# Root of the norm applied to the results in six norms, spread modulation units, loads reordered at the start, mix heads with scaling ahead and one recurrence chunk per head

## The chip, the core and the metric

One core of one Trainium2 chip runs the whole program in one launch. The metric is the time of an execution in device microseconds (us). Five engines work from instruction streams of their own and wait for one another through semaphores: TensorE (PE; its weight loads are PEld), VectorE (DVE), ScalarE (ACT), GpSimd (POOL) and SyncE (SP), which here issues every DMA.

## The reference

256 tokens of width 1024 in float32 pass two networks one after the other. The first has two layers of: a SwiGLU feed-forward block; a mixing block (a gated linear recurrence of 1024 channels beside forgetting attention with 8 heads of 128, merged by sigmoid gates); a second SwiGLU block; and a gated projection of a side input ("PLE"). Each of the four starts with an RMS norm:

```python
def rms_norm(x, g):
    xf = x.astype(jnp.float32)
    y = xf * lax.rsqrt(jnp.mean(xf * xf, axis=-1, keepdims=True) + EPS)
    return (y * g.astype(jnp.float32)).astype(x.dtype)

for i in range(DEPTH):                       # DEPTH = 2
    x = x + 0.5 * swiglu_ffn(rms_norm(x, ffn1_norm[i]), ffn1_w_in[i], ffn1_w_out[i])
    h = rms_norm(x, mix_norm[i])
    ...
    merged = jax.nn.sigmoid(ga + mb_a) * ya + jax.nn.sigmoid(gb + mb_b) * yb
    x = x + merged @ w_o[i]
    x = x + 0.5 * swiglu_ffn(rms_norm(x, ffn2_norm[i]), ffn2_w_in[i], ffn2_w_out[i])
    gate = jax.nn.sigmoid(rms_norm(x, ple_norm[i]) @ ple_w_gate[i] + ple_b_gate[i])
    x = x + gate * (p[i] @ ple_w_proj[i])
```

The second network (two layers on 256 tokens and, at first, 256 context tokens) has feed-forward blocks, a convolution block and windowed attention. Its norms are scaled, shifted and gated by modulation vectors: silu(c) times the matrices ada_w, of 1024 x 9216 for each layer. These products depend on no token, so the kernel does them along the way.

## The kernel before, in words

Activations lie transposed, channels on partitions and tokens along the free axis: Xx is x as 8 chunks (kc) of 128 channels x 256 tokens. The weights are cut into **units** of 256 output columns, 1 MB each (the loop variable u, with u.k its number). A float32 product is made of three: a weight w is split into wh (ACT copies raw to the reduced format, L1048, helper hi) and wl = raw - wh (DVE, L1443, helper lo), an activation likewise into Hh and Hl (or Fh and Fl), and PE adds wh*Hh, wh*Hl and wl*Hh (L560 to L562, helper linear). A unit has two tiles t of 128 columns, and for 256 tokens takes 48 matmuls of 256 columns.

raw has four slots, filled by SP in the order of units; wh and wl have two buffers, by the unit's parity, so hi(u+2, t) waits until PE has done tile t of unit u. The results of a unit are in two banks of PSUM, again by parity.

The order on each engine is written out by hand: every engine has one straight program, and in it each unit is a turn, with hi(u+2), lo(u+2) placed around what the engine does with the results of u.

- A **feed-forward** block is 34 units in three groups: 8, 8 and 6 units G (gate and up columns side by side) each followed by 4 units O (down projection). For a unit G, ACT takes the tanh of the gate tile (L1118), DVE multiplies (L1436, L1520) into Pp, ACT and DVE split that into Fh and Fl (L1129, L1536).
- A **norm** comes between blocks. ACT squares x by pairs of chunks, DVE adds them, PE sums over channels with a matrix of ones (L596), ACT takes the square root (L1091), DVE the reciprocal (L1453), PE spreads it over partitions (L617) into PSUM bank 4. Then, chunk by chunk, DVE writes x * gain * root (L1436), ACT copies it to Hh (L1103), DVE makes Hl (L1481), and PE's first unit of the next block starts with the first chunk.
- Modulation is done in 18 **batches** of 4 units of ada_w. Each takes 16 matmuls (L634) straight from raw. In the kernel before, a batch sits at one place: eight of the first nine in a norm (norm_sums), around the sums and the root, or at the first head; their 4 MB take all four slots of raw, and the next block's second unit (Unit(after + 1), "held") is loaded and split only after them. Before the first one, c has to be turned and passed through silu.
- The **mix heads**: 8 steps st. In each, PE does tile 0 of a unit of the merge gates, head_values(st - 2) (L803), spread(st) (L783: the inverse norms of q and k of head st, spread over partitions into bank 4), tile 1, turn_probs(st - 1) (L769) and head_scores(st) (L793 to L795). DVE scales Q and K of head st by bank 4 (L1733, L1734; semaphore qkn_done), masks and takes maxima of the scores (L1737 to L1744), normalises after ACT's exp (L1216), and in steps 0 to 3 runs the recurrence of two chunks: multiply (L1436), scan (L1759), times the gelu gate (L1762; y_done), ACT copies to Fh (L1236), DVE makes Fl (L1766). ACT ends the step with the tanh of the merge gates (L1240) and begins the next with hi.

```python
for st in range(HEADS):                                   # PE, L800 on
    u = Unit(k + 20 + st)
    linear(u, part(Hh, T), part(Hl, T), T, tiles=(0,))
    ...
    spread(st)
    linear(u, part(Hh, T), part(Hl, T), T, tiles=(1,))
    if st >= 1:
        turn_probs(st - 1)
    head_scores(st)
```

- **PLE** is four pairs of units: a gate unit and a projection unit (2 chunks deep, 12 matmuls). ACT takes the gate's tanh from PSUM (L1275), DVE combines gate and projection and adds to x (L1436 twice), ACT squares x for the next norm (L1081).
- At the **start** SP issues the tokens, then 28 loads of parameters, then the weights.

Of the kernel before, what the change touches and what calls it, by code (L numbers as in the profile page):

```python
# [33 lines left out]
P = 128  # L34
T = 256
# [35 lines left out]
BATCH_AFTER = tuple(k for l in range(DEPTH) for k in ((K_LAYER,) if l else ()) + (  # L71
    l * K_LAYER + K_MIX, l * K_LAYER + K_GATES, l * K_LAYER + K_FFN2, l * K_LAYER + K_PLE)) + (
    K_SECOND, K2_CONV, K2_CONV + 4, K2_PW2, K2_FFN2, K2_L1, K2_KV, K2_KV + 5, K2_FFN4)
assert BATCH * len(BATCH_AFTER) == 2 * MOD_UNITS


def batches_before(k):
    return sum(after < k for after in BATCH_AFTER)


class Unit:
# [3 lines left out]
    def __init__(self, k):  # L85
        self.k = k
        self.slot = k % 4
        self.par = k % 2
        self.raw = k + BATCH * batches_before(k)
# [7 lines left out]
    def held(self):  # L97

        return self.k - 1 in BATCH_AFTER or self.k == K2_WO + 1
# [4 lines left out]


    def batch_member(self):

        b = batches_before(self.k) - 1
        return (b, self.k - BATCH_AFTER[b] - 1) if b >= 0 and self.k - BATCH_AFTER[b] <= BATCH else None

    def raw_free(self):
        return 2 * self.k + 2
# [22 lines left out]
class ModUnit:  # L135
# [3 lines left out]
    def __init__(self, b, m):  # L139
        self.b, self.m = b, m  # L140
        self.place = BATCH_AFTER[b] + 1 + m
        self.raw = self.place + BATCH * b
        self.slot = self.raw % 4
        self.l, self.index = divmod(BATCH * b + m, MOD_UNITS)
# [4 lines left out]
    def raw_free(self):  # L149
        return Unit(self.place).raw_free()  # L150

    def done(self):
        return BATCH * self.b + self.m + 1

# [51 lines left out]
def build(nc, A, out):  # L206
# [12 lines left out]
    with ctx:  # L219
# [43 lines left out]
        tiny = sb("tiny", [P, 64])  # L263
        S1 = sb("S1", [P, 3, C, 2])
# [42 lines left out]
        sqa_done = sem("sqa_done")  # L307
        rs_done, rb_done = sem("rs_done"), sem("rb_done")
# [70 lines left out]

        def head_row(what, h):  # L380
# [3 lines left out]
        def mod_bank(b):  # L384

            return 7 if BATCH_AFTER[b] in (K_GATES, K_LAYER + K_GATES, K2_CONV + 4, K2_KV + 5) else 5

        def mod_rows(b):

            if BATCH_AFTER[b] == K2_KV + 5:  # L390
                return Vb[:, 1, 0:T]
            return Ss[:, T:2 * T] if BATCH_AFTER[b] in (K_GATES, K_LAYER + K_GATES) else Rr[:, T:2 * T]
# [5 lines left out]
        def _(sp):  # L398
# [11 lines left out]
            for r, name in ((R_FFN1, "ffn1_norm"), (R_MIX, "mix_norm"), (R_MERGE, "merge_b"), (R_CONVB, "conv_b"),  # L410
# [1665 lines left out]
```

## Time and profile before

| | us |
|---|---|
| median of 3 runs | 3329.41 (3328.5 to 3331.13) |
| the profiled execution's own time | 3330.55 |
| its span | 3328.8 |
| PE busy in the span | 3181.1 (96%) |
| PE weight loads busy | 2799.8 (84%) |
| DVE busy | 1913.6 (57%) |
| ACT busy | 1346.4 (40%) |
| mean granted clock of TensorE | 0.975 |

The span is what the profiler recorded from first to last instruction; the execution's own time is 1.75 us more. Busy time is the sum over an engine's instructions, overlaps counted once. A matmul counts as busy at whichever of the two clocks it runs, so a share of 96% does not say that 4% is all there is to gain.

### The profile page before, as it was taken

To read this page: it belongs to the slowest core of one execution; us is meant where nothing else is said; L and a number is where in the kernel's file an instruction comes from. 1 tells how busy PE (TensorE), PEld (TensorE's weight loads), DVE (VectorE), ACT (ScalarE), POOL (GpSimd) and SP (SyncE) were. 2 spreads that over 40 slices of the span, in tenths; PEclk is the share of its full clock that TensorE was granted. 3 is DMA by queue.
4 is the path that set the end of the run, shared out by engine and by line. 5 is a ranking of instruction groups with operands and counts; after the bars stand their busy time and mean duration, and the time that the engine had idled before them with its cause. 6 is when DMAs were issued, how large, how long until landed. Compare 5 with 4: busy or idle time off the path is not lost.

```text
span 3328.8 us, 49855 instructions
## 1 busy us (share of the span) xinstructions
PE 3181.1 (96%) x21085; PEld 2799.8 (84%) x21085; DVE 1913.6 (57%) x2983; ACT 1346.4 (40%) x2046; POOL 2.3 (0%) x6
## 2 busy tenths in 40 slices
PE   7999899998999899998999999899999999999999
PEld 7999799998998889997888866578887888874898
DVE  5567656556557666556434379853335433455555
ACT  4445344445444444445322242432223222337544
POOL 0000000000000000000000000000000000000000
PEclk8999899999999999998999999999999999999999
DMA  6675437666665537657333343253334333242563
GB/s 194 181 209 159 159 126 213 185 195 199 188 201 173 180 102 208 187 166 220 102 102 89 89 127 101 88 140 89 102 92 124 114 89 101 89 140 76 165 184 108
DMA packets 671175, 478.86 MB, mean 144 GB/s; under 512 B 21487, under 2 KB 670057, under 8 KB 670953
## 3 DMA queue, kind: packets, MB, share of 16 engines
q1 hardware_dynamic: 670953, 475.68, 47.8%
q8 instruction: 166, 2.72, 0.3%
q14 instruction: 56, 0.46, 0.0%
HBM read 474.57 MB, written 1.05 MB: 143 GB/s over the span
## 4 chain that ended last, share of the span: by engine, by line
PE 80%; DVE 10%; ACT 4%; DVEq 3%; DMA 1%; issue 1%; SPq 0%; ACTq 0%
PE ps L560 24%; PE ps L562 24%; PE ps L561 24%; DVE Pp L1436 3%; DVE wl L1443 3%; DVEq L1895 2%; ACT wh L1048 2%; PE ps L634 1%; PE ps L999 1%; DMA raw<-in_ada_w 1%; DVEq L1486 1%; PE ps L976 1%; DVE Hl L1436 1%; PE ps L617 1%; ACT L1060 1%
## 5 line engine op out<-in xcount | busy, mean ns | idle before, releaser
L1443 DVE TENSOR_TENSOR wl<-raw,wh 128x1024 fp32r<-128x1024 f32 x780 | 951.2, 1224 | 920.2 <-ACT wh L1048 919.5
L1048 ACT ACTIVATE wh<-raw 128x1024 fp32r<-128x1024 f32 x780 | 816.5, 1057 | 1477.6 <-PE ps L562 1410.6
L560 PE MATMUL ps<-Hh,wh 128*128 128x256 f32 (+1 forms) x4048 | 1305.1, 322 | 44.4 <-DVE Hl L1436 13.8
L562 PE MATMUL ps<-Hh,wl 128*128 128x256 f32 (+1 forms) x4048 | 1287.3, 318 | 0.0
L561 PE MATMUL ps<-Hl,wh 128*128 128x256 f32 (+1 forms) x4048 | 1287.1, 318 | 0.0
L560 PEld LDWEIGHTS ps<-Hh,wh 128*128 128x128 f32 x4048 | 785.7, 194 | 111.0 <-issue 37.8
L561 PEld LDWEIGHTS ps<-Hl,wh 128*128 128x128 f32 x4048 | 786.1, 194 | 49.6 <-issue 2.4
L562 PEld LDWEIGHTS ps<-Hh,wl 128*128 128x128 f32 x4048 | 784.8, 194 | 48.2
L560 PE MATMUL ps<-Fh,wh 128*128 128x256 f32 (+1 forms) x1824 | 582.0, 319 | 13.2 <-DVE Fl L1805 7.7
L561 PE MATMUL ps<-Fl,wh 128*128 128x256 f32 (+1 forms) x1824 | 580.7, 318 | 0.0
L562 PE MATMUL ps<-Fh,wl 128*128 128x256 f32 (+1 forms) x1824 | 580.6, 318 | 0.0
L560 PEld LDWEIGHTS ps<-Fh,wh 128*128 128x128 f32 x1824 | 348.9, 191 | 37.6 <-DVE Fl L1805 8.2
L562 PEld LDWEIGHTS ps<-Fh,wl 128*128 128x128 f32 x1824 | 349.0, 191 | 23.4
L561 PEld LDWEIGHTS ps<-Fl,wh 128*128 128x128 f32 x1824 | 349.0, 191 | 23.2
L1520 DVE TENSOR_TENSOR Pp<-Ss,ps 128x256 f32<-128x256 f32 (+1 forms) x176 | 91.8, 521 | 157.1 <-PE ps L562 154.3
L1436 DVE SCALAR_TENSOR_TENSOR Pp<-Vb,par,Pp 128x512 f32<-128x512 f32 x155 | 109.8, 748 | 6.7 <-issue 0.9
L1436 DVE SCALAR_TENSOR_TENSOR Xx<-ps,G,Xx 128x256 f32<-128x256 f32 x112 | 52.3, 479 | 90.1 <-PE ps L562 90.0
L1129 ACT ACTIVATE Fh<-Pp 128x256 fp32r<-128x256 f32 (+1 forms) x176 | 85.0, 483 | 30.3 <-DVE Pp L1520 30.3
L1536 DVE TENSOR_TENSOR Fl<-Pp,Fh 128x256 fp32r<-128x256 f32 (+1 forms) x176 | 91.2, 518 | 0.0
L1436 DVE SCALAR_TENSOR_TENSOR Ss<-Tt,ps 128x256 f32<-128x256 f32 (+1 forms) x176 | 90.6, 515 | 0.0
L634 PE MATMUL ps<-raw,cs 128*32 128x256 f32 x1152 | 72.8, 393 | 10.8 <-DMA raw<-in_ada_w 10.8
L1118 ACT ACTIVATE Tt<-ps 128x256 f32<-128x256 f32 (+1 forms) x176 | 78.5, 446 | 0.0
(273 smaller groups left out, 1895.4 us busy)
## 6 DMA issues: line engine op xcount, KB each, us to landing
raw<-in_ffn_w_in SPq DMA_DIRECT2D x176, 512.0 KB, 5.2
raw<-in_ffn_wi SPq DMA_DIRECT2D x176, 512.0 KB, 5.2
raw<-in_ada_w SPq DMA_DIRECT2D x144, 512.0 KB, 4.5
raw<-in_w_in SPq DMA_DIRECT2D x112, 512.0 KB, 4.8
raw<-in_ffn_w_out SPq DMA_DIRECT2D x64, 512.0 KB, 4.3
raw<-in_ffn_wo SPq DMA_DIRECT2D x64, 512.0 KB, 4.3
raw<-in_ffn_w_out SPq DMA_DIRECT2D x32, 384.0 KB, 3.5
raw<-in_ffn_wo SPq DMA_DIRECT2D x32, 384.0 KB, 3.6
```

The costliest lines, as they stand in the source:

```text
L560: nc.tensor.matmul(o, wh[:, u.par, kc, w], xh(kc), start=(kc == 0), stop=False)
L561: nc.tensor.matmul(o, wh[:, u.par, kc, w], xl(kc), start=False, stop=False)
L562: return nc.tensor.matmul(o, wl[:, u.par, kc, w], xh(kc), start=False, stop=(kc == kc_n - 1))
L634: mm = nc.tensor.matmul(ps[32 * j:32 * j + 32, mod_bank(b), 0:256], cs[:, kc, 2 * (BATCH - 1 - m):2 * (BATCH - 1 - m) + 32], raw[:, u.slot ...
L1048: nc.scalar.activation(tile_of(wh[:, u.par], t), tile_of(raw[:, u.slot], t), ACT.Copy) \
L1118: nc.scalar.activation(Tt[:, u.par, 0:n], bank(u, 0, n), ACT.Tanh, scale=0.5) \
L1129: nc.scalar.activation(dst, src, ACT.Copy).then_inc(fh_done, 1)
L1436: return V.scalar_tensor_tensor(out=o, in0=in0, scalar=scalar, in1=in1, op0=op0, op1=op1)
L1443: V.tensor_tensor(tile_of(wl[:, u.par], t), tile_of(raw[:, u.slot], t), tile_of(wh[:, u.par], t).bitcast(F32), ALU.subtract).then_inc(lo_d ...
L1520: V.tensor_tensor(Pp[:, u.par, 0:n], Ss[:, 0:n], bank(u, 1, n), ALU.mult) \
L1536: V.tensor_tensor(o, p, h.bitcast(F32), ALU.subtract).then_inc(f_done, 1)
L1895: dve.drain()
```

## The change

Six things are changed; nothing in the second network's blocks is, but for names.

1. **Six norms deferred** (0, 2, 3 of each layer's 0 to 3, that is the norms ahead of both feed-forward blocks and of PLE; the norm ahead of mix stays). The split is made of x * gain without the root: ACT unscaled_high (two copies with a scale, after each pair's squares), DVE unscaled_low (two instructions, a turn later). PE begins the next block on these; the sums go ahead of chunk 4 of its first unit and the spreading of the root ahead of chunk 7 (norm_between). ACT copies the root to SBUF, and DVE multiplies results by it: in each unit G two more multiplications (before the tanh, and before the product), in PLE one per gate unit. PLE's tanh now reads what DVE wrote (L2015).
2. **Modulation units spread**: five of the first nine batches go as single units between units of the feed-forward blocks (MEMBER_AT), their copy, turn and keep one, two and three units after the last.
3. **Start**: one load of ffn1's gains as a column (gain0, 4-byte elements), then the weights of units 0 to 3, then the parameters; PE turns the parameters after unit 1, DVE copies them before unit 2, and c is prepared before unit 4.
4. **PLE's side input** is turned and split during the last group of the feed-forward block before it.
5. **Mix heads, scaling ahead**: spread(st + 1) stands after tile 1 of step st, ahead of turn_probs and head_scores(st).
6. **Recurrence**: one chunk in each of the eight steps in place of two in each of the first four; its Fl a step later (scanned_low), the last one after the steps.

```diff
+def batch_places():
+    out = []
+    for l in range(DEPTH):
+        k = l * K_LAYER
+        out.append(tuple(k + j for j in ((3, 5, 7, 9) if l else (8, 10, 13, 15))))
+        if l:
+            out.append(tuple(k + j for j in (15, 17, 19, 21)))
+        out += [(k + K_MIX,) * BATCH, (k + K_GATES,) * BATCH, tuple(k + K_FFN2 + j for j in (3, 5, 7, 9))]
...
+            with nc.allow_non_contiguous_dma(reason="a column of gains"):
+                sp.dma_start(gain0[:], A["ffn1_norm"][0].rearrange("(c p) -> p c", p=P)).then_inc(gain_in, 16)
...
+                        if u.k == 4:
+                            load_params()
...
                     linear(u, part(Hh, T), part(Hl, T), T, tiles=(0,))
...
-                    spread(st)
+                    if st == 0:
+                        spread(0)
                     linear(u, part(Hh, T), part(Hl, T), T, tiles=(1,))
+                    if st + 1 < HEADS:
+                        spread(st + 1)
                     if st >= 1:
                         turn_probs(st - 1)
                     head_scores(st)
...
+            def last_add(norm_i, i, u):
+
+                hi(u.later(2), 0)
+                if i == 3:
+                    squares(norm_i, i, T, u)
+                    unscaled_high(norm_i, i)
+                    hi(u.later(2), 1)
+                else:
+                    hi(u.later(2), 1)
+                    squares(norm_i, i, T, u)
+                    unscaled_high(norm_i, i)
...
-                    if st < 4:
-                        for j in (2 * st, 2 * st + 1):
-                            act.wait_ge(y_done, l * C + (j + 1))
-                            nc.scalar.activation(Fh[:, 0, j, :], Pp[:, j % 2, T:2 * T], ACT.Copy).then_inc(yh_done, 1)
+                    act.wait_ge(y_done, l * C + (st + 1))
+                    nc.scalar.activation(Fh[:, 0, st, :], Pp[:, st % 2, T:2 * T], ACT.Copy).then_inc(yh_done, 1)
...
                     hi(u.later(2), 0)
-                    hi(u.later(2), 1)
-                    act.wait_ge(mm_done, u.mm_done(1))
+                    act.wait_ge(banks_free[u.par], u.read_out())
                     for t in range(2):
                         r = R_PLEB + 2 * j + t
-                        ins = nc.scalar.activation(Pp[:, j % 2, t * T:(t + 1) * T], bank(u, t, T), ACT.Tanh, scale=0.5,
-                                                   bias=half[:, r:r + 1])
-                    ins.then_inc(banks_free[u.par], 1)
+                        a = Pp[:, j % 2, t * T:(t + 1) * T]
+                        ins = nc.scalar.activation(a, a, ACT.Tanh, scale=0.5, bias=half[:, r:r + 1])
+                    ins.then_inc(ple_tanh, 1)
+                    hi(u.later(2), 1)
...
+                            r = inverse_root(norm)
+                            dve.wait_ge(mm_done, u.mm_done(0))
+                            V.tensor_tensor(Ss[:, 0:n], bank(u, 0, n), r, ALU.mult).then_inc(a_done, 1)
+                            lo(u.later(2), 0)
+                            done = fi * FC + g * 8
+                            dve.wait_ge(tanh_done, done + (i + 1))
+                            stt(Ss[:, 0:n], Tt[:, u.par, 0:n], 1.0, Ss[:, 0:n], ALU.add, ALU.mult)
+                            dve.drain()
+                            V.tensor_tensor(Ss[:, 0:n], Ss[:, 0:n], r, ALU.mult)
+                            dve.drain()
+                            dve.wait_ge(mm_done, u.mm_done(1))
+                            V.tensor_tensor(Pp[:, u.par, 0:n], Ss[:, 0:n], bank(u, 1, n), ALU.mult) \
+                                .then_inc(banks_free[u.par], 1)
...
-                        for j in two_chunks:
-                            V.tensor_tensor_scan(Pp[:, j % 2, 0:T], decay[:, j, :], Xc[:, j, :], 0.0, ALU.mult, ALU.add)
...
+                    V.tensor_tensor_scan(Pp[:, st % 2, 0:T], decay[:, st, :], Xc[:, st, :], 0.0, ALU.mult, ALU.add)
+                    dve.drain()
+                    V.tensor_tensor(Pp[:, st % 2, T:2 * T], Pp[:, st % 2, 0:T], Gb[:, st, :], ALU.mult) \
+                        .then_inc(y_done, 1)
+                    if st >= 1:
+                        scanned_low(st - 1)
+                scanned_low(HEADS - 1)
```

What moves on the engines, at the two places that matter most. Each row is one instruction: line, operation, written and read tiles, shape of the output, and what it waits for.

PE in a head step, from the end of tile 1 of the merge-gate unit to tile 0 of the next. Before (L769 turns the probabilities, L793 to L795 are the scores):

```order
L562 MATMUL ps<-Hh,wl 128x256
L769 MATMUL ps<-co,Tt 128x128 [waits pn_done]
L769 MATMUL ps<-co,Tt 128x128 x2
L793 MATMUL ps<-QK 128x128 [waits qkn_done]
L794 MATMUL ps<-tt_r,picks 128x128
```

and with the change (L881 is spread, L867 turn_probs, L891 the scores):

```order
L615 MATMUL ps<-Hh,wl 128x256
L881 MATMUL ps<-rqs,picks 128x256 [waits qkn_done]
L881 MATMUL ps<-rqs,picks 128x256 x3
L867 MATMUL ps<-co,Tt 128x128 [waits pn_done]
L867 MATMUL ps<-co,Tt 128x128 x2
L891 MATMUL ps<-QK 128x128 [waits qkn_done]
```

The wait for qkn_done now stands ahead of the four spreading matmuls and of the turning, where it stood behind the turning.

ACT in head step 5, between the tanh of two merge gates. Before (L1048 is hi, L1211 head_out, L1207 the turned probabilities, L1216 exp):

```order
L1240 ACTIVATE Gb<-ps,half 128x256
L1048 ACTIVATE wh<-raw 128x8x128 [waits mm_done,raw_full1]
L1211 ACTIVATE Fh<-ps 128x256 [waits pv_done]
L1048 ACTIVATE wh<-raw 128x8x128 [waits mm_done]
L1207 ACTIVATE Tt<-ps 128x384 [waits tr_done]
L1216 ACTIVATE Tt,tiny<-Tt,tiny 128x128 [waits nmax_done]
L1216 ACTIVATE Tt,tiny<-Tt,tiny 128x256
L1240 ACTIVATE Gb<-ps,half 128x256 [waits mm_done]
```

and with the change:

```order
L1380 ACTIVATE Gb<-ps,half 128x256
L1142 ACTIVATE wh<-raw 128x8x128 [waits mm_done,raw_full1]
L1353 ACTIVATE Fh<-ps 128x256 [waits pv_done]
L1142 ACTIVATE wh<-raw 128x8x128 [waits mm_done]
L1349 ACTIVATE Tt<-ps 128x384 [waits tr_done]
L1358 ACTIVATE Tt,tiny<-Tt,tiny 128x128 [waits nmax_done]
L1358 ACTIVATE Tt,tiny<-Tt,tiny 128x256
L1376 ACTIVATE Fh<-Pp 128x256 [waits y_done]
```

The copy of the recurrence's result (L1376), with its wait for y_done, now stands ahead of the merge gates' tanh in steps 4 to 7 too, where nothing stood; in steps 0 to 3 it is one copy in place of two.

## Rows read from the trace of the kernel before

**Rows 1.** The page: busy engines; waits of PE: total, times, longest

```profile
PE 3181.1 (96%) x21085; PEld 2799.8 (84%) x21085; DVE 1913.6 (57%) x2983; ACT 1346.4 (40%) x2046; POOL 2.3 (0%) x6
...
PE ps L634 <- DMA raw<-in_ada_w: 10.8, 8, 4.8
```

**Rows 2.** Stretches: length, busy PE, PEld, DVE, ACT, POOL (instructions), clock, DMA share, GB/s

```profile
0.00:28.55 28.55, 8.73 (x65) 7.70 (x66) 11.73 (x28) 9.25 (x13) 2.30 (x6) 0.73 0.82 217
28.55:33.30 4.75, 4.75 (x22) 4.75 (x23) 4.29 (x11) 2.08 (x5) 0.00 (x0) 0.50 0.63 151
36.40:210.00 173.60, 173.60 (x1449) 173.60 (x1448) 104.89 (x139) 77.86 (x108) 0.00 (x0) 1.00 0.64 185
389.10:467.40 78.30, 70.96 (x470) 64.88 (x469) 51.79 (x131) 33.29 (x77) 0.00 (x0) 0.90 0.30 97
440.40:467.40 27.00, 27.00 (x201) 24.85 (x201) 16.25 (x42) 13.09 (x30) 0.00 (x0) 1.00 0.35 118
1156.20:1232.60 76.40, 68.60 (x471) 62.29 (x470) 51.87 (x132) 33.19 (x77) 0.00 (x0) 0.93 0.33 107
538.40:554.30 15.90, 13.01 (x157) 11.12 (x157) 9.37 (x22) 8.45 (x16) 0.00 (x0) 0.89 1.05 271
738.80:783.40 44.60, 38.44 (x357) 34.86 (x360) 31.24 (x44) 26.86 (x41) 0.00 (x0) 0.96 0.61 193
783.40:804.90 21.50, 16.27 (x157) 13.33 (x156) 11.81 (x28) 10.25 (x20) 0.00 (x0) 0.76 1.05 283
```

**Rows 3.** Timeline of PE at the start (start, us, engine, line, tiles); DMA issues

```profile
6.40 3.46 PE L686 MATMUL ps<-co,QK 128*128 128x128 f32 x16 [6.40 <-DMA QK<-in_x]
...
wf<-in_w_in SPq DMA_DIRECT2D x2, 32.0 KB, 5.2
```

**Rows 4.** The chain that ended last: start, us, engine, line; two modulation units

```profile
538.40 1.86 PE ps L634 x32
```

**Rows 5.** Timeline of ACT and DVE in PLE of layer 0, pairs 2 and 3

```profile
775.01 0.82 ACT L1275 ACTIVATE Pp<-ps,half 128x256 f32<-128x256 f32 x2
775.72 2.00 ACT L1048 ACTIVATE wh<-raw 128x1024 fp32r<-128x1024 f32 x2
780.04 0.63 ACT L1081 ACTIVATE Tt<-Xx 128x512 f32<-128x512 f32 x1 [2.31 <-DVE Xx L1436]
...
778.55 0.68 DVE L1436 SCALAR_TENSOR_TENSOR Ss<-Pp,ps 128x512 f32<-128x512 f32 x1
```

**Rows 6.** Timeline of DVE in a unit G: first instruction of its turn

```profile
58.01 1.23 DVE L1443 TENSOR_TENSOR wl<-raw,wh 128x1024 fp32r<-128x1024 f32 x1 [1.38 <-ACT wh L1048]
```

**Rows 7.** Timeline of DVE and ACT, head step 3 and the start of step 4

```profile
428.56 0.29 DVE L1737 TENSOR_TENSOR Tt<-ps,co 128x128 f32<-128x128 f32 x1 [1.93 <-PE ps L795]
...
431.23 0.17 DVE L1752 RECIPROCAL tiny<-tiny 128x2 f32<-128x2 f32 x1 [0.39 <-ACT Tt L1216]
...
431.94 1.26 DVE L1759 TENSOR_TENSOR_SCAN Pp<-decay,Xc 128x256 f32<-128x256 f32 x2
433.28 0.76 DVE L1762 TENSOR_TENSOR Pp<-Pp,Gb 128x256 f32<-128x256 f32 x2
...
436.20 1.23 DVE L1443 TENSOR_TENSOR wl<-raw,wh 128x1024 fp32r<-128x1024 f32 x1 [1.25 <-ACT wh L1048]
...
440.42 0.29 DVE L1737 TENSOR_TENSOR Tt<-ps,co 128x128 f32<-128x128 f32 x1 [0.59 <-PE ps L795]
...
433.74 0.75 ACT L1236 ACTIVATE Fh<-Pp 128x256 fp32r<-128x256 f32 x2 [2.54 <-DVE Pp L1762]
434.40 0.82 ACT L1240 ACTIVATE gateA<-ps,half 128x256 f32<-128x256 f32 x2
```

**Rows 8.** Timeline of PE in a head step: the spreading

```profile
443.84 0.71 PE L783 MATMUL ps<-rqs,picks 128*128 128x256 f32 x4
```

**Rows 9.** Busy time by stretch: a wait of PE among the heads, and what follows

```profile
422.70:425.50 2.80, 0.03 (x1) 0.00 (x0) 2.22 (x5) 2.14 (x4) 0.00 (x0) 1.00 0.00 0
425.50:428.50 3.00, 2.95 (x9) 1.84 (x9) 1.13 (x1) 0.00 (x0) 0.00 (x0) 0.57 0.24 55
438.50:440.30 1.80, 1.80 (x8) 1.15 (x8) 1.23 (x1) 0.45 (x2) 0.00 (x0) 1.00 0.00 0
```

More of the change, by code:

```diff
@@ L70, with ring_order @@
 BATCH = 4
[L71 to L78, printed above, removed]
+def batch_places():
[6 more added lines that the diff above has]
+        out += [(k + K_MIX,) * BATCH, (k + K_GATES,) * BATCH, tuple(k + K_FFN2 + j for j in (3, 5, 7, 9))]
+    return out + [(k,) * BATCH for k in (
+        K_SECOND, K2_CONV, K2_CONV + 4, K2_PW2, K2_FFN2, K2_L1, K2_KV, K2_KV + 5, K2_FFN4)]
+BATCHES = batch_places()
+PLACES = [k for places in BATCHES for k in places]
+assert len(PLACES) == 2 * MOD_UNITS and PLACES == sorted(PLACES)
+BATCH_AT = {places[0]: b for b, places in enumerate(BATCHES) if places[0] == places[-1]}
+SPREAD = {b: places for b, places in enumerate(BATCHES) if places[0] != places[-1]}
+MEMBER_AT = {k: (b, m) for b, places in SPREAD.items() for m, k in enumerate(places)}
+P_TURN_AT, P_HIGH_AT, P_LOW_AT = ({l * K_LAYER + K_FFN2 + j: l for l in range(DEPTH)} for j in (26, 28, 29))
+COPY_AT = {places[-1] + 1: b for b, places in SPREAD.items()}
+TURN_AT = {places[-1] + 2: b for b, places in SPREAD.items()}
+KEEP_AT = {places[-1] + 3: b for b, places in SPREAD.items()}
+def ring_order():
+    out = []
+    for k in range(K2_END):
+        out.append((k, None))
+        out += [(None, i) for i, place in enumerate(PLACES) if place == k]
+    return out
+RING = ring_order()
+RAW_OF_UNIT = {k: r for r, (k, i) in enumerate(RING) if i is None}
+RAW_OF_MOD = {i: r for r, (k, i) in enumerate(RING) if i is not None}
 class Unit:
@@ L263, in build @@
         tiny = sb("tiny", [P, 64])
+        gain0 = sb("gain0", [P, C])
         S1 = sb("S1", [P, 3, C, 2])
@@ L665, in ffn @@
                     for j, (kind, i, u) in enumerate(units):
-                        if kind == "G":
+                        if kind == "G" and norm is not None:
+                            uh, ul = unscaled(norm)
+                            first = g == 0 and i == 0
+                            if first and norm == 0:
+                                linear(u, part(uh, n, 1), part(ul, n, 1), n, ready=u_ready(norm), together=False,
+                                       between=norm_between(0, 12, 15))
+                            else:
+                                linear(u, part(uh, n, 1), part(ul, n, 1), n, ready=u_ready(norm) if first else None,
+                                       between=norm_between(norm) if first else {})
+                        elif kind == "G":
                             linear(u, part(Hh, n), part(Hl, n), n, ready=h_ready(hn) if i == 0 else None)
@@ L1525, in ffn @@
                             stt(x, pair(u), 0.25, x, ALU.mult, ALU.add).then_inc(banks_free[u.par], 1)
+                            if last and i == 3 and deferred(after):
+                                unscaled_low(after, i)
                         else:
@@ L2046, in _ @@
                 lo(u.later(2), 1)
-            norm(14, T, 13, gain(2), shift(1, 2), K2_FFN4)
+            norm(14, T, 7, gain(2), shift(1, 2), K2_FFN4)
             gate_const(1, 2)
```

457 lines of the change are left out of this document (281 added, 176 removed).

## The prediction

> **What bounds the kernel.** I read the page's busy engines first, then the busy time by stretch, then the waits of PE, and at the places that wait longest the timelines of PE, DVE and ACT. PE is busy 96% of the span [rows 1], so at most 148 us are idle, to which half clock adds. In the middle of a feed-forward block there is nothing to gain: from 36.4 to 210 us PE is never idle at clock 1.00 (2.4 GHz; 0.50 is 1.2 GHz), 1449 matmuls in 173.6 us, 120 ns each [rows 2], so a unit of 48 takes 5.8 us. Time is lost where these streams break: the start, the norms, the mix heads. The reader should see these three in [rows 2], and that the last three head steps (440.4 to 467.4) lose nothing: 27.00 busy of 27.0, 9.0 us a step.
>
> **The change, part by part.** I sum against the profiled execution, 3330.55, which is 1.1 above the median.
>
> *Start.* Before, the first unit begins at 28.55 and does 22 matmuls by 33.3 at clock 0.50 (216 ns each), the other 26 at 120 ns: it ends at 36.4 [rows 2]. Now it needs tokens, turned from 6.4 to 9.9 [rows 3], and its weights, which go ahead of the parameters but behind gain0. A transfer of 32 KB in 1024 small pieces, wf, takes 5.2 us to land [rows 3]; gain0 has as many pieces, so I let it land at 8 to 9, and unit 0 a megabyte later, 3.8 us at the 271 GB/s of a norm [rows 2], at 12 to 13. Two splits (1.05 and 1.2 us) put the first matmul at 14.5. Its 48 matmuls at the half clock take 10.4, sums and root some 2: the unit ends at 27, 9.4 earlier. The parameters' turning, hidden before, now costs some 1.5. Gain 7.9; bounds 4 (parameters land after unit 1) and 11 (nothing waits, clock full early).
>
> *Norms ahead of the second feed-forward block, one a layer.* From the last matmul ahead of it to the next unbroken stream it takes 15.9 us, with PE busy for 13.0 and the clock at 0.89 [rows 2]: 2.9 idle and 0.11 x 15.9 = 1.7 by the clock, 4.6 lost. Now PE starts unit 0 at once. The last pair's x (0.7), squares (0.6), two scaled copies (0.8, as two of L1275) and as much again for the low halves [rows 5] are there some 3.2 us after the end, with signals between, and chunk 6 is wanted after 36 matmuls, 4.3; the root (two instructions on 64 columns, together under 1 us, behind a split each) is there at about 5, wanted at about 5.5. I take the whole 4.6 twice: gain 9.2; bounds 5 and 11.
>
> *Norm ahead of PLE, PLE, norm after it.* Layer 0: 44.6 and 21.5 us [rows 2], 66.1 in all, of which by the same count (6.2 + 1.8 and 5.2 + 5.2) 18.4 are lost. This looks like the best place, but behind the norm stands a loop. Before, a pair takes 8.0 us (PE 7.2). Now DVE first multiplies the gate by the root, and only then ACT takes its tanh. From the end of that multiplication: tanh 0.75, three splits of 1.0 on ACT (a fourth waits for PE), two of 1.2 on DVE behind them, two combinations of 0.7, ACT's squares 0.6 and scaled copies 0.8, the next pair's split 1.05 and 1.2, the next multiplication 0.65 [rows 5, 6]: 10.0 us, 10.8 with the low halves and 11.4 with the adding of squares. Three such gaps make 32 us against 24. Worked through, unit 0 of layer 1 ends 55 us after the end of the feed-forward block; before it ended 65.4 after, and 8 or 9 of that (eight modulation units of 0.93 [rows 4], and turnings) have moved elsewhere. Gain 2. In layer 1 (no scaled copies: 9.2, 9.2, 9.8) the same count gives nothing. Bounds for both together: -3 (a loss) and +8.
>
> *Extra DVE work in 88 units G.* Two multiplications, 0.4 us each by the width of L1436 and L1520. DVE waits 1.38 us ahead of each turn [rows 6], so they fit: nothing, as long as DVE keeps under 5.8 us a unit.
>
> *Spread modulation.* The PE work is the same. Their waits for DMA, 10.8 us in 8 [rows 1], are mostly in the norms counted above. Three megabytes now must come in each 12.5 us (two units and one member) through four slots, and the third load can start only when the member before it is used: 3 x 3.8 is 11.4 at the 271 GB/s of [rows 2], and with one or two us from issue to the first byte it is about as long as there is. I take 0.1 us for each of 20 members, loss 2; bounds 0 and 10.
> The Trainium skill (DMA: Bandwidth & Descriptors, Specifications) puts the limit of HBM for one core at about 358 GB/s. By that, an estimate, three megabytes need 8.8 us, the members never wait, and this term is 0. The trace stays below it where the transfers are the longest queue, 271 to 283 GB/s over a whole norm [rows 2], so the rule and the rows differ, and the sum goes by the rows.
>
> *Heads.* This decides. Between scores in steps 3 and 4: DVE starts on the scores at 428.56, has 1/sum at 431.23, scans from 431.94, multiplies from 433.28, ACT copies from 433.74, takes the gates' tanh from 434.40, splits, and only then DVE's first split of the next step starts, at 436.20; next come Q and K, the scores on PE, and DVE again at 440.42 [rows 7]: **11.86 us**, a loop over DVE, ACT and PE, against PE's own 9.0. The change takes out one scan and with it 0.64 of the wait (first product 0.7 after the scan's start, not 1.34), and one copy of 0.33: -0.97. But the spreading for the next head (0.6 [rows 8]) and the turning (0.3) now wait for qkn_done with the scores behind them, where they were done before it came: +0.9. A step is 11.8 us again, and all eight have a chunk, so that the last three go from 9.0 to 11.8. Seven steps: 82.4 us, against 78.3 and 76.4 [rows 2]: +4.1 and +6.0. Behind the steps, the first product of the recurrence's output wants chunks 6 and 7, which are there 5.2 us after the last scores in place of 2.2: +3.1 a layer. Scores of head 0 stand behind spread(1): +0.6 a layer. Together **+17.5**. Bounds: -28 if steps were as PE alone makes them, 9.0; nothing speaks for more on DVE.
>
> *Clock in the heads.* PE now idles 2.8 us in each step. Before, 2.80 us without PE (422.7 to 425.5) are followed by a stretch at 0.57, in which the scores take 3.0 us in place of 1.8 [rows 9]. With spreading and turning in that stretch it is 2 at worst, every step: +28. After a slow stretch PE's rest of the step is longer, the idle time shorter; so I take every second step at 1.0: +7.
>
> Sum: 3330.55 - 7.9 - 9.2 - 2 + 2 + 17.5 + 7 = 3338, less 1.1 for the median: **3337**. Undone, the same sum without heads would be 3312.
>
> **Rivals.**
> 1. *Forecast: the heads' loop, with some slow clock.* For: the 11.86 is built from rows, and ACT's order puts the copy ahead of the split in each step. 0.42; 3331 to 3345.
> 2. *The loop, clock stays up.* The first slow stretch does not come because single waits of 2.8 us are not enough. Against: after 422.7 it came. 3330, no change by my bound of 0.2%, or 6.7 us, about what a measurement can tell. 0.25.
> 3. *PLE runs as PE alone would, 7.2 us a pair.* The tanh on SBUF and early copies hide; both layers gain some 25 in place of 2: 3337 - 23 = 3314, **faster**. Decides if ACT's squares and copies are not ahead of the next split's need. Against: the order on ACT. 0.12.
> 4. *Heads as PE alone makes them, 9.0 us a step.* Scaling ahead takes Q and K off the loop. It would need DVE to multiply before the split, which it doesn't. 17.5 + 7 turn into about -28: 3285. 0.06.
> 5. *Slow clock in every head step, or members late by 0.5 us each.* +21 or +8 on the forecast: 3345 to 3358. 0.15.
>
> **Numbers.** Range 3312 to 3355: it takes in rivals 1 to 3 and most of 5, and leaves out 4 and the end of 5, about 0.15 to 0.2. Faster by over 0.2% (below 3322.8): 3, 4 and some luck at the start, 0.22. Within: rival 2 and the lower part of 1, 0.33. Slower (above 3336.1): most of 1 and 5, 0.45.
>
> **What would show it.** Right: in the changed profile the stretch of 8 head steps is 85 to 95 us, its steps even at 11.8 or more, each with PE waiting 2 to 3 us at the spreading (L881) for DVE; the last three no longer full; stretches with clock below 1.00 among them. PLE pairs 9 to 11.5 us apart. First feed-forward matmul near 14.5. No idle time ahead of the second feed-forward blocks. Wrong: head steps of 9 to 10 us; PLE pairs near 8; waits of PE for ada_w or of ACT for raw between units G.

## The result and the profile after

The changed kernel takes 3349.85 us (median of 5 runs, 3347.85 to 3351.85) beside 3329.75 for the kernel before on the same chip: ratio 1.0051, 95% interval 1.0040 to 1.0062, so **slower**, by 20 us from median to median and by 17 us (13 to 21) by the ratio. Its profiled execution took 3351.85, its span 3350.1, at a mean granted clock of 0.975. The forecast was 3337, with 0.45 on slower. One execution of all the runs, the profiled one of the experiment with the parameters first, ran at a mean clock of 0.64 and took 4532.68 us, and no ratio in this document counts it.

The page and the waits of PE after (waited for: us in total, times, longest):

```profile
PE 3197.5 (95%) x21085; PEld 2802.4 (84%) x21085; DVE 1968.6 (59%) x3119; ACT 1355.1 (40%) x2052; POOL 2.3 (0%) x6
...
PE ps L613 <- DVE wl L1581: 18.5, 10, 5.3
PE ps L881 <- DVE QK L1942: 15.8, 10, 2.5
...
PE ps L613 <- DVE Pp L2015: 9.9, 6, 2.3
...
PE ps L691 <- DMA raw<-in_ada_w: 5.8, 4, 3.1
```

Against [rows 1], PE has the same 21085 matmuls and 16 us more busy time. The mean clock is 0.975 in both kernels, so it is not half clock everywhere: 13.7 of the 16 lie between the first scores and the first merged pair of the two layers, where the clock is 0.90 and 0.91 and was 0.94 and 0.96 before. The waits for ada_w fell from 10.8 to 5.8. The wait for Q and K stood at the scores before (L793) and has grown; it now stands mostly at the spreading (L881), with 4.2 left at the scores:

```profile
PE ps L793 <- DVE QK L1734: 13.4, 7, 3.2
```

New is the wait of PLE's next unit for the multiplication by the root (L2015).

The busy time by stretch, for the changed kernel (columns as in [rows 2]):

```profile
78.40:152.70 74.30, 74.30 (x641) 72.15 (x640) 46.79 (x72) 30.82 (x41) 0.00 (x0) 1.00 0.85 241
...
388.60:473.50 84.90, 74.65 (x466) 66.95 (x466) 50.45 (x127) 33.50 (x76) 0.00 (x0) 0.86 0.28 89
...
532.50:548.90 16.40, 16.40 (x139) 16.40 (x138) 12.46 (x18) 10.76 (x16) 0.00 (x0) 1.00 0.62 182
734.60:751.70 17.10, 14.52 (x132) 13.95 (x130) 13.12 (x19) 10.53 (x17) 0.00 (x0) 1.00 0.43 139
765.40:798.80 33.40, 24.03 (x159) 23.38 (x158) 23.43 (x30) 18.92 (x28) 0.00 (x0) 0.80 0.62 181
```

In order: units of the first block with three modulation members (single units of ada_w) among them; the mix heads from the first scores to the last; the last units ahead of the second feed-forward block; the last group of that block; PLE. The heads take 84.9 us where [rows 2] have 78.3, at a clock of 0.86 for 0.90.

To see where the 21.3 us of span went, I took one kind of instruction that both kernels have, DVE's adding of a finished pair to x (and the first scores of the heads), and compared its start times. The last column is what the stretch that ends there adds. Members of modulation batches that moved are noted, since they carry their own time with them.

| ends at | before | after | added |
|---|---|---|---|
| first unit O, layer 0 | 84.7 | 78.4 | -6.3 |
| end of the first block (4 members more) | 221.0 | 219.8 | +5.1 |
| first scores | 389.2 | 388.6 | +0.6 |
| first merged pair | 523.1 | 532.5 | **+10.0** |
| fourth merged pair | 538.4 | 548.9 | +1.1 |
| first unit O of block 2 (4 members of the norm gone, 3 spread ones in) | 602.6 | 607.2 | -5.9 |
| first O of its last group (1 spread member in) | 727.8 | 734.6 | +2.2 |
| last O | 738.9 | 751.0 | **+5.3** |
| first PLE pair (4 members less) | 761.9 | 765.4 | -8.6 |
| fourth PLE pair | 785.6 | 798.8 | **+9.7** |
| first unit O, layer 1 (4 members of the norm gone, 3 spread ones in) | 853.2 | 857.1 | -9.3 |
| end of the first block (5 members more) | 989.5 | 1000.2 | +6.8 |
| first scores | 1156.3 | 1168.5 | +1.5 |
| first and fourth merged pair | 1288.3, 1303.6 | 1311.6, 1328.0 | **+11.1**, +1.1 |
| block 2: first O, first O of last group (members as in layer 0) | 1369.2, 1494.5 | 1386.3, 1513.7 | -7.3, +2.1 |
| last O | 1505.5 | 1530.1 | **+5.4** |
| first and fourth PLE pair (4 members less ahead of the first) | 1528.0, 1552.4 | 1544.5, 1572.0 | -8.1, +3.1 |
| end of the span | 3328.8 | 3350.1 | +1.7 |

The heads, from first scores to first merged pair, add 21.1. Next come the last four units of block 2 with 10.7, of which the prediction said nothing. The rest sums to -10.5: what start, norms and PLE gain is half of what the heads lose.

**Why a head step is still 11.75 us.** Timelines of DVE and ACT in head step 5 of the changed kernel:

```profile
449.91 0.29 DVE L1945 TENSOR_TENSOR Tt<-ps,co 128x128 f32<-128x128 f32 x1 [2.68 <-PE ps L893]
...
453.30 0.68 DVE L1962 TENSOR_TENSOR_SCAN Pp<-decay,Xc 128x256 f32<-128x256 f32 x1
454.06 0.42 DVE L1964 TENSOR_TENSOR Pp<-Pp,Gb 128x256 f32<-128x256 f32 x1
454.40 0.42 DVE L1926 TENSOR_TENSOR Fl<-Pp,Fh 128x256 fp32r<-128x256 f32 x1
456.64 1.23 DVE L1581 TENSOR_TENSOR wl<-raw,wh 128x1024 fp32r<-128x1024 f32 x1 [1.82 <-ACT wh L1142]
...
461.66 0.29 DVE L1945 TENSOR_TENSOR Tt<-ps,co 128x128 f32<-128x128 f32 x1 [0.89 <-PE ps L893]
```

```profile
454.51 0.42 ACT L1376 ACTIVATE Fh<-Pp 128x256 fp32r<-128x256 f32 x1 [1.96 <-DVE Pp L1964]
454.84 0.82 ACT L1380 ACTIVATE Gb<-ps,half 128x256 f32<-128x256 f32 x2
455.55 1.06 ACT L1142 ACTIVATE wh<-raw 128x1024 fp32r<-128x1024 f32 x1
```

ACT sits idle for 1.96 us until the product of the scan is there, only then takes the gates' tanh, for which everything had long been ready, and only then the split for which DVE waits 1.82 in turn. It is the loop of [rows 7] with one chunk less, and PE sees it here (timeline of PE at the end of step 4):

```profile
446.15 0.74 PE L881 MATMUL ps<-rqs,picks 128*128 128x256 f32 x4 [2.44 <-DVE QK L1942]
446.72 0.49 PE L867 MATMUL ps<-co,Tt 128*128 128x128 f32 x3
...
447.93 1.22 PE L891 MATMUL ps<-QK 128*128 128x256 f32 x2
...
458.91 0.74 PE L881 MATMUL ps<-rqs,picks 128*128 128x256 f32 x4 [0.49 <-DVE QK L1942]
```

After the wait of 2.44 the scores run at half clock (1.22 for what takes 0.70 at 460.50), and that step is 12.76. In the next one the half clock lasts into PE's other work (449.9 to 461.7: 11.31 us busy, granted clock 0.81), which merely fills the wait, of which 0.49 is left: 11.75. A step that is bound by the loop hides the slow clock everywhere but in the matmuls of the loop itself, between the wait and the end of the scores.

**Why the last units of block 2 are slower.** ACT and DVE in the last group, changed kernel:

```profile
740.37 0.64 ACT L1175 ACTIVATE Tt<-Xx 128x512 f32<-128x512 f32 x1 [1.73 <-DVE Xx L1574]
740.90 0.90 ACT L1183 ACTIVATE Hh<-Xx,par 128x256 fp32r<-128x256 f32 x2
741.70 2.00 ACT L1142 ACTIVATE wh<-raw 128x1024 fp32r<-128x1024 f32 x2
```

```profile
742.78 1.23 DVE L1581 TENSOR_TENSOR wl<-raw,wh 128x1024 fp32r<-128x1024 f32 x1 [1.32 <-ACT wh L1142]
743.92 0.69 DVE L1599 TENSOR_TENSOR Tt<-Tt 128x512 f32<-128x512 f32 x1
744.53 0.87 DVE L1574 SCALAR_TENSOR_TENSOR Hl<-Xx,par,Hh 128x256 fp32r<-128x256 f32 x2
745.32 0.69 DVE L1574 SCALAR_TENSOR_TENSOR Xx<-ps,Xx 128x512 f32<-128x512 f32 x1
```

Here a unit has 6 chunks, which is 36 matmuls or 4.3 us of PE. ACT squares and scales the pair as soon as x is there, with the next split queued behind; DVE waits 1.32 for that split and only then comes to the next x. DVE's 4.4 us of work and its wait of 1.3 make 5.7.

### The profile page after: what moved, and what is told of

It reads as the page before. It is cut to its first block, busy times and chain, and to the rows that moved or that the text cites. A ratio compares the mean times of both kernels' runs of the same rounds, so it can differ in the third digit from the quotient of the medians.

```text
span 3350.1 us, 50063 instructions
## 1 busy us (share of the span) xinstructions
PE 3197.5 (95%) x21085; PEld 2802.4 (84%) x21085; DVE 1968.6 (59%) x3119; ACT 1355.1 (40%) x2052; POOL 2.3 (0%) x6
## 4 chain that ended last, share of the span: by engine, by line
PE 77%; DVE 11%; ACT 6%; DVEq 3%; issue 2%; DMA 1%; SPq 0%; ACTq 0%
PE ps L613 23%; PE ps L615 22%; PE ps L614 22%; DVE wl L1581 3%; DVE Pp L1574 3%; ACT wh L1142 2%; DVEq L2106 1%; PE ps L691 1%; PE ps L1093 1%; DVE Hl L1574 1%; PE ps L1070 1%; DVE Xx L1574 1%; PE ps L674 1%; DMA raw<-in_w_in 1%; PE ps L891 1%
## 5 line engine op out<-in xcount | busy, mean ns | idle before, releaser
L613 PE MATMUL ps<-Fh,wh 128*128 128x256 f32 (+1 forms) x3200 | 978.2, 306 | 17.4 <-DVE Fl L2128 5.6
L614 PE MATMUL ps<-Fl,wh 128*128 128x256 f32 (+1 forms) x3200 | 972.3, 304 | 0.0
L615 PE MATMUL ps<-Fh,wl 128*128 128x256 f32 (+1 forms) x3200 | 972.0, 304 | 0.0
L613 PE MATMUL ps<-Hh,wh 128*128 128x256 f32 (+1 forms) x2672 | 913.0, 342 | 48.8 <-DVE Hl L1574 13.8
L614 PE MATMUL ps<-Hl,wh 128*128 128x256 f32 (+1 forms) x2672 | 895.3, 335 | 0.0
L615 PE MATMUL ps<-Hh,wl 128*128 128x256 f32 (+1 forms) x2672 | 894.7, 335 | 0.0
L613 PEld LDWEIGHTS ps<-Fh,wh 128*128 128x128 f32 x3200 | 615.4, 192 | 52.8 <-issue 15.6
L614 PEld LDWEIGHTS ps<-Fl,wh 128*128 128x128 f32 x3200 | 615.7, 192 | 23.1
L615 PEld LDWEIGHTS ps<-Fh,wl 128*128 128x128 f32 x3200 | 615.5, 192 | 23.3
L613 PEld LDWEIGHTS ps<-Hh,wh 128*128 128x128 f32 x2672 | 519.1, 194 | 118.3 <-issue 30.1
L614 PEld LDWEIGHTS ps<-Hl,wh 128*128 128x128 f32 x2672 | 519.3, 194 | 48.7 <-issue 2.4
```

The costliest lines, as they stand in the source:

```text
L613: nc.tensor.matmul(o, wh[:, u.par, kc, w], xh(kc), start=(kc == 0), stop=False)
L614: nc.tensor.matmul(o, wh[:, u.par, kc, w], xl(kc), start=False, stop=False)
L615: return nc.tensor.matmul(o, wl[:, u.par, kc, w], xh(kc), start=False, stop=(kc == kc_n - 1))
```

## The experiments

Ratios are to the kernel before, run beside each kernel on the same chip. A difference of ratios times 3330 gives the us by which I compare kernels of different chips.

**The heads as before.** In the changed kernel, PE's spreading goes back between the two tiles, and both chunks back to the first four steps:

```diff
-                    if st + 1 < HEADS:
-                        spread(st + 1)
+                    spread(st)
-                    act.wait_ge(y_done, l * C + (st + 1))
+                    if st < 4:
+                        for j in (2 * st, 2 * st + 1):
```

> The changed kernel (3349.85 us) with the mix heads' order and recurrence of before. Loop theory: by the ledger of the two traces the heads cost 10.6 us in layer 0 and 12.6 in layer 1, so this runs at 3349.85 - 23.2 = 3326.6 (3325 to 3329), its last three head steps 9.0 us apart. Rival, the heads only take up time that would be lost behind them anyway (attention, merge, norm): 3338 or more. In both cases the last four units of the second feed-forward block stay 5.0 to 5.7 us apart, and the PLE pairs 10.7 to 11.4.

Measured 3327.99, ratio 0.9986 (0.9975 to 0.9997): 21.6 less than the changed kernel. The last two head steps are 9.04 and 9.03, as expected, and the heads' time is not given back behind them. The two edits of the heads are the whole loss of the change.

**Only the spreading back.** The first half of that edit.

> The changed kernel with the spreading of a head back between the two halves of a gate unit; still one chunk of the recurrence in every step. Loop theory: spreading and turning lay 0.9 us in the loop, 14 steps, and 0.6 for each first head: -13.8, so 3336 (3334 to 3339), steps of 10.9 where the clock is full. Rival A, PE has the time anyway and the chunk is the whole price: 3349. Rival B, the shorter wait also ends the slow clock, 7 us more: 3329.

Measured 3334.18, ratio 1.0008 (0.9998 to 1.0017): 14.3 less, where 13.8 were expected. A step in busy time by stretch:

```profile
430.10:441.00 10.90, 9.25 (x68) 8.30 (x68) 7.22 (x18) 4.79 (x11) 0.00 (x0) 1.00 0.30 96
```

Four steps in a row are 10.94 to 10.95, for the 10.9 expected: spreading and turning behind qkn_done are worth what their durations say, 11.75 - 10.94 = 0.81. Both rivals fall: the spreading has a price (A), and there is no gain of 7 us on top of it (B).

**Only the recurrence back.** The second half.

> The changed kernel with two chunks in each of the first four head steps again, the spreading as in the change (behind the step before). Loop theory: four steps of 12.8 instead of 11.8, three of some 9.9, and 3.1 less behind the last head, so -4.9 a layer: 3340 (3337 to 3344). Rival, the place of the spreading is the whole loss: 3350 or more, with late steps of 11.8 as now.

Measured 3334.34, ratio 1.0007 (0.9998 to 1.0016): 14.7 less, where 10 were expected. Steps with two chunks are 12.65 at best, as expected (12.8), and up to 14.7. Their clock is 0.77 to 0.87, but it is 0.81 in the step of 12.65 too, so the clock alone does not tell them apart. But without a chunk they are 9.37, not 9.9: I had put the 0.9 of the late spreading on PE's own 9.0, and only a third of it shows. Behind the last head 3.7 and 3.4 go (3.1 expected).

The two halves do not add up: 14.3 and 14.7 alone make 29.0, and together they brought 21.6 (the intervals of the four ratios leave this difference 7 us either way). The traces fit it: once late steps have no chunk, they are near PE's own 9.0 and the place of the spreading costs them a third of a microsecond (9.37 for 9.04), where it costs 0.81 in a step with a chunk.

**The heads' edits on the kernel before.**

> The kernel before (3329.75 us) with the two edits of the mix heads alone (spreading for the next head behind the step, one chunk of the recurrence in each of eight steps). Loop theory: they cost the same here as in the changed kernel, 23.2: 3353 (3350 to 3356). Rival, the heads were slow in the changed kernel because of something that the other edits brought (transfers of the spread units, buffers): under 3345.

Measured 3355.07, ratio 1.0064 (1.0049 to 1.0079), 21.3 more than the kernel before. From first scores to first merged pair it takes 146.5 and 143.5, for 133.9 and 131.9 before: +24.2 in these stretches. The two edits carry their loss with them, whatever the norms do.

**One chunk a step, but ACT's copy out of the loop.** Spreading in its old place, and on ACT (scanned_high(j) is the copy of chunk j, with its wait):

```diff
                     hi(u.later(2), 0)
                     if st >= 2:
                         head_out(st - 2)
+                    if st >= 1:
+                        scanned_high(st - 1)
                     hi(u.later(2), 1)
...
                     head_exp(st)
-                    act.wait_ge(y_done, l * C + (st + 1))
-                    nc.scalar.activation(Fh[:, 0, st, :], Pp[:, st % 2, T:2 * T], ACT.Copy).then_inc(yh_done, 1)
+                    if st == HEADS - 1:
+                        scanned_high(st)
```

> The changed kernel with the spreading back in its old place and ACT's copy of a chunk put behind the first split of the next step, so that the gates' tanh and that split no longer wait for the scan; one chunk in every step. Loop theory: the way from scores to scores becomes 9.05 us, as long as PE's own 9.0: head steps 9.0 to 9.3 from the second on, no slow clock, 7 steps in 64 where they take 84.9, 42 less in both layers: 3308 (3304 to 3314), faster than both kernels. Rival, DVE's own row of instructions (7.2 us busy and its waits for scores and exponentials) sets the step: steps of 10.9 as with the spreading alone, 3336.

Measured 3313.6, ratio 0.9942 (0.9921 to 0.9963), 36.3 less than the changed kernel and faster than the kernel before. Busy time by stretch, a step and all eight:

```profile
385.30:453.20 67.90, 65.54 (x470) 59.72 (x471) 49.62 (x127) 33.20 (x76) 0.00 (x0) 0.97 0.37 120
425.80:434.90 9.10, 9.10 (x68) 8.16 (x67) 7.21 (x20) 4.79 (x11) 0.00 (x0) 1.00 0.34 115
```

DVE and ACT do the same work in such a step as in the one of 10.9 above (7.2 and 4.8 us), and PE is never idle. The order on ACT made the loop, not the amount of work. One step of each layer stays long, the third (the second interval between scores): 13.15 and 11.66, which is part of why 36.3 came and not the 42 expected. PE's waits in layer 0 name its cause, the only one in the stretch:

```profile
PE ps L901 <- DVEq L1664: 2.4, 1, 2.4
```

This is head_values(0) waiting for DVE to keep the gate modulation, which stands behind step 1's scan on DVE; the kernel before has this wait too, and it stands there in a step of 14.64.

**PLE's order.** On ACT, for a pair j: both halves of the gate unit's split, then squares and scaled copies of pair j - 1, the first half of the next split, the tanh, the second half.

> The changed kernel with ACT's order in the PLE pairs changed: both halves of a gate unit's split first, squares and scaled copies of the pair before behind them, the first half of the next split ahead of the tanh. Loop theory: the pairs are then as long as DVE's own work, 8.3 us in layer 0 (10.7, 11.4, 11.3 now) and 7.5 in layer 1 (9.1, 9.7, 8.6): -8.5 and -5, so 3336 (3333 to 3340). Rival, the transfers for the short PLE units or the slow clock hold the pairs: 3347 or more. Pairs near 10 would mean that another wait has taken its place.

Measured 3331.46, ratio 0.9995 (0.9986 to 1.0005): 18.6 less, more than the 13.5 expected and below the range. The four pairs of layer 0:

```profile
761.60:787.30 25.70, 23.00 (x199) 22.13 (x197) 23.26 (x30) 18.84 (x28) 0.00 (x0) 1.00 0.83 234
```

25.7 us for 33.4, at full clock, DVE busy 23.3 of them and PE 23.0: DVE is the bound in layer 0 now, near the count of 8.3 a pair (9.3, 7.9, 8.5). In layer 1 the pairs are 7.7, 7.8 and 6.0. The pairs give 7.7 and 6.0 (8.5 and 5 expected); the rest is that the first pair is ready 1.4 and 2.0 earlier, which I had not counted, and the way from the last one of layer 1 to the end is 1.9 shorter. Of that only 0.7 comes within 45 us; the first experiment also has 1.6 less there, without any edit of PLE, so the rest is not shown to be PLE's.

**The last units of block 2.** On ACT, squares and scaled copies of pair i - 1 between the two halves of unit i's split.

> The changed kernel with ACT's squares and scaled copies of a pair put between the two halves of the next unit's split, in the last four units of the second feed-forward block. Loop theory: those units, now 5.0, 5.7 and 5.7 us apart, go to DVE's own 4.5: -2.9 a layer, 3344 (3342 to 3346). Rival, DVE's added low halves (0.87) and the adding of squares are the whole price: spacing stays over 5.3, 3349.

Measured 3340.74, ratio 1.0025 (1.0015 to 1.0034): 8.7 less, more than the 5.8 expected and below the range. The units are 3.7, 4.6 and 4.3 apart in both layers, and in layer 0 PE is never idle there (12.50 of 12.50 us); DVE's wait for the split is 0.22 where it was 1.32:

```profile
741.27 1.23 DVE L1588 TENSOR_TENSOR wl<-raw,wh 128x1024 fp32r<-128x1024 f32 x1 [0.22 <-ACT wh L1142]
```

**Parameters first again,** ahead of all weights.

```diff
-                        if u.k == 4:
-                            load_params()
+            load_params()
```

> The changed kernel with the parameters' transfers ahead of the first weights again, nothing else. If the earlier weights bring the gain at the start (6.3 us by the trace), this gives it back: 3356 (3354 to 3360), the first feed-forward matmul near 25 to 28 in place of 13.8. Rival, the deferred norm alone brings it and the parameters are small beside a megabyte of weights: 3350 to 3351, first matmul under 16.

Measured 3358.68 (3356.68 to 3359.99 without the profiled execution), ratio 1.0074 (1.0057 to 1.0090): 7.7 more. Its profile is that of the execution of 4532.68 us; up to 20.8 us its granted clock is 1.00, and only that part is read, on ACT and PE:

```profile
18.27 1.06 ACT L1142 ACTIVATE wh<-raw 128x1024 fp32r<-128x1024 f32 x1 [6.88 <-DMA raw<-in_ffn_w_in]
```

```profile
20.80 0.55 PE L613 MATMUL ps<-Fh,wh 128*128 128x256 f32 x1 [10.69 <-issue]
```

The first matmul is at 20.8, not at 25 to 28 as I expected, and at 13.81 in the changed kernel. So of the 14.7 us by which the change brings it forward from 28.55 [rows 2], the order of the loads is 7.0, and the other 7.7 are left for the deferred root and what else moved at the start. In time, the 7.7 of this run are as much as the 6.3 that the start gained by the table. But the two ratios leave anything from 1 to 14 us, so that the loads are the whole gain is not shown.

**The three repairs together**, then **the gate modulation kept earlier** (on DVE, keep_modulation behind Q and K of step 1), then also **the last chunk taken in the last but one step**:

> The changed kernel with the three repairs together: spreading in its old place and ACT's copy of a chunk behind the next split, ACT's order in the PLE pairs, ACT's order in the last four units of the second feed-forward block. Loop theory: three separate loops in three places, so their gains of 36.2, 18.4 and 9.1 add up: 3349.85 - 63.7 = 3286 (3282 to 3291), faster than both kernels by over 40 us. Rival, the gains overlap (a faster stage is given back in the next, as transfers come late): 3295 or more.

> The kernel with the three repairs, and DVE's keeping of the gate modulation (behind which PE's values of head 0 wait, 2.4 us in the third head step) put behind Q and K of the second step. Theory: the third step, 13.2 us in layer 0 and 11.7 in layer 1, becomes 9.0 to 9.3 like the others: -4.1 and -2.6, so 3279 (3276 to 3283). Rival, the slow clock there has another cause: -1 at most, 3285.

> The same, and the last chunk of the recurrence taken in the last but one step. Theory: behind the last scores the first product of the recurrence's output has its chunks 5 us earlier (60.4 us from the last scores to the first merged pair now, 55.3 in the kernel before), against some 1.5 us more of DVE in that step: -3.5 a layer, 3272 (3269 to 3276). Rival, the second chunk puts the step back on the loop and slows the clock: -1 a layer or less, 3277 or more.

Measured 3289.45 (ratio 0.9863, 0.9847 to 0.9880), 3281.13 (0.9843, 0.9828 to 0.9858) and 3279.73 (0.9840, 0.9825 to 0.9855). The three gains of 36.3, 18.6 and 8.7 make 63.6 together; 62.6 were measured. The third step became 9.39 and 9.05. The last chunk brought half of what it should by the traces: it gains 3.1 and 2.8 behind the last scores and costs 1.0 and 1.4 in its step; by the ratios it is 1 us, outside the expected range. In layer 1 the first step took 11.59 in place of 9.09, for the clock alone, as PE is busy in all of it (heads of layer 0, then that step):

```profile
383.40:449.30 65.90, 64.37 (x470) 58.23 (x470) 51.34 (x129) 33.62 (x77) 0.00 (x0) 1.00 0.40 127
1128.40:1140.00 11.60, 11.60 (x70) 10.94 (x71) 6.72 (x19) 4.51 (x10) 0.00 (x0) 0.76 0.44 143
```

The intervals overlap from one kernel to the next. For the early keeping the traces show the step that it shortens, and its slowest execution (3283.69) is below the fastest without it (3284.88). For the last chunk neither is so, and I take it as not shown to be faster.

**The last heads on the kernel before.**

> The kernel before with the mix heads of the last run alone (one chunk in each step but two in the last but one, ACT's copy behind the next split, modulation kept earlier; spreading where it always was); all norms, the start and PLE as before. Theory: from the first scores to the first merged pair layer 0 took 133.9 us before and 123.3 in the last run, layer 1 132.0 and 124 to 126: -17.6, so 3312 (3309 to 3316). The rest of the way to 3280, some 32 us, is then what deferring the norms is worth once ACT's order no longer eats it. Rival, the repaired heads profit from the other edits (transfers, clock): 3318 or more.

Measured 3312.02, ratio 0.9938 (0.9925 to 0.9952). The heads take 123.0 and 123.2 from first scores to first merged pair, at a clock of 0.99 and 1.00. The eight steps of layer 0:

```profile
387.80:453.40 65.60, 64.39 (x470) 58.23 (x471) 51.40 (x130) 33.62 (x77) 0.00 (x0) 1.00 0.39 124
```

So of the 1.6% by which the best version beats the kernel before, 0.62 come from the heads. The other 0.98, 33 us, are by difference the worth of start, norms, PLE and spread modulation once ACT's orders are mended; as the change came, the same edits brought 0.14 (first experiment).

## Why the prediction was right, and where it was not

The forecast, rival 1, said slower for the reason that held, but 13 us too little (3337 for 3349.85). Trace against trace, the sum had +7.4 and measured is +21.3. By its own steps:

- **Start, -7.9.** Measured -6.3; first matmul 13.81 for 14.5. Right within 1.6, and inside its bounds of 4 and 11.
- **Norms ahead of block 2, -4.6 each.** -5.9 and +2.2 in layer 0, -7.3 and +2.1 in layer 1. The two stretches together hold the same four members in both kernels, so they are added: -3.7 and -5.2, -8.9 in all for -9.2. No idle time is left in 532.5 to 548.9, and behind it, where the norm stood, 0.2 us:

```profile
548.90:607.00 58.10, 57.93 (x527) 55.36 (x527) 38.15 (x63) 28.56 (x42) 0.00 (x0) 1.00 0.68 205
```

- **PLE.** Pairs were to be 10.0, 10.8 and 11.4 us in layer 0, and are 10.7, 11.3 and 11.3 (9.2, 9.2, 9.8 in layer 1, and 9.1, 9.7, 8.6). From the last O of block 2 to the end of the next first block, where the eight members moved out of the norms come back, layer 0 gives -8.6 + 9.7 - 9.3 + 6.8 = -1.4, for -2. The members came back dearer than they left (next but one point), so this agreement is in part luck.
- **Extra DVE work in units G, nothing.** Right: 74.30 of 74.30 us busy in a stretch with 641 matmuls.
- **Spread members, +2 for waits.** Not one wait of PE for ada_w stands in the feed-forward blocks, the waits fell by half, and the stretch with members moves 241 GB/s. Here the rule that the prediction set beside the rows, the Trainium skill's limit of about 358 GB/s for one core (DMA: Bandwidth & Descriptors, Specifications), gave the right term, 0. But the rate was not 358: the weights move at 293 when they queue, and soon after the queue is nearly empty:

```profile
98.00:101.00 3.00, 3.00 (x27) 3.00 (x26) 0.83 (x2) 0.67 (x1) 0.00 (x0) 1.00 1.19 293
105.00:109.00 4.00, 4.00 (x42) 3.28 (x41) 3.50 (x8) 2.60 (x4) 0.00 (x0) 1.00 0.06 21
```

  So the 271 of the prediction was not far off; what failed in this term is the one or two us that it added to the 11.4. And "the PE work is the same" was wrong. Four members cost 5.1 in the first block where they took 3.7 in a norm, with no wait. The chain of work that ended last shows it, in the first block (start, us, engine, line):

```profile
89.11 1.00 PE ps L691 x16
90.11 0.32 PE ps L613
...
132.97 0.35 PE ps L702 x4
133.32 0.22 PE ps L613
```

  A member is 1.00, and the full matmul behind it takes 0.32 in place of 0.12: 1.20 each, where two together took 1.86 in the norm [rows 4]. With the turning, 0.35 and 0.10, that makes 5.25 for four. Five batches were spread, some 7 us that the sum did not have; they are inside the figures above and hide how much the norms gained.
- **Heads, +17.5, and +7 for the clock.** Of fourteen steps, six are 11.74 to 11.80 for the 11.8 forecast, three (two first, one last) 10.9 to 11.5, and five 12.5 to 13.7. These five exceed 11.75 by 6.1 in all. The table has 21.1 and, with the way to the first scores, 23.2; the first experiment gave 21.6 and the fourth 21.3 (24.2 in its stretches). So the 24.5 of the prediction are the right size. The waits at the spreading are at most 2.5 and 1.6 in the mean, less than the 2 to 3 I named, since half clock fills them.
- **What failed: the step on PLE, in where it begins.** It costed scaled copies and low halves behind the last pair ahead of block 2 and between PLE's pairs. The same copies are made, for PLE's own norm, in the last group of block 2, and the sum has no term for them, though a unit there is only 4.3 us of PE. That is +10.7 by the table, and 8.7 came back with the order mended. The prediction's sum and the table are 13.9 apart. The rest of that is 2.2 in the merged pairs and 1.7 behind the last PLE pair, whose causes were not tried, 2.5 by which start, norms and PLE of layer 0 fell short, and in the other direction 1.3 in the heads and 1.9 in the waits of the members.

Rival 3, PLE as PE alone, came true only with another order on ACT, and in layer 0 only in part: the pairs are 8.6 in the mean there, DVE's work, and 7.2 in layer 1, which is PE's own time. Rival 4, heads at 9.0, was given 0.06 because the change did not take anything out of ACT's row; with the copy out of it and the spreading back in its place, steps are 9.02 to 9.29 but for the one that waits for the gate modulation.

## What to carry to other kernels

When an engine that is 40% busy stands between two that wait for each other, look at the order of its instructions, not at its load: a copy of 0.42 us that waits for a late product held back a tanh and a split that were ready, and moving it was worth 22 us (second against fifth experiment), more than the whole change lost. When work is added to "an engine that has time", go through every kind of unit in which it lands, the shortest first. And an edit that looks like an evening out (one chunk in eight steps for two in four) makes all steps as long as the loop, if one chunk is enough to close it.

## Not expected of the hardware

Token and constant loads came in at 420 GB/s in one stretch of the changed kernel, where the weights behind them move at 290:

```profile
3.50:5.50 2.00, 0.00 (x0) 0.00 (x0) 0.00 (x0) 0.00 (x0) 0.00 (x0) 1.00 1.02 420
6.50:20.00 13.50, 9.40 (x51) 8.74 (x52) 9.82 (x17) 9.14 (x15) 0.00 (x0) 0.87 1.19 290
```

So the 358 GB/s of the prediction is not a ceiling here. The Trainium skill (HBM Reference, Specifications (TRN2)) gives it as the share of a core whose neighbour is busy too, and about 425 for a core that streams alone; the 420 agree with that. What holds the weights at 290 these runs do not show.

And half clock came in a head step in which PE was never idle: 11.60 busy of 11.60 at 0.76 above, where the same step of the kernel without the last chunk's move took 9.09. What PE did just before does not settle which steps it strikes. In that kernel PE waited 1.37 us for the first Q and K, and the clock fell in the scores behind it; in the kernel before with the last heads it waited 1.32 at the same place in layer 0, and the clock stayed (for each, PE's first matmul behind the wait and the busy time of the stretch behind it):

```profile
1125.99 0.49 PE L891 MATMUL ps<-QK 128*128 128x128 f32 x2 [1.37 <-DVE QK L1954]
...
1126.00:1128.40 2.40, 2.40 (x9) 1.48 (x9) 1.07 (x1) 0.00 (x0) 0.00 (x0) 0.74 1.10 348
...
385.83 0.49 PE L793 MATMUL ps<-QK 128*128 128x128 f32 x2 [1.32 <-DVE QK L1741]
...
385.80:387.80 2.00, 1.97 (x9) 1.31 (x10) 1.14 (x2) 0.00 (x0) 0.00 (x0) 1.00 1.10 348
```
